# Scores of the local attention issued in pairs of an even and an odd head

## The reference

```
q = q.reshape(B, NC, CHUNK, SWA_KV_HEADS, G, SWA_HEAD_DIM)
...
s = jnp.einsum('bcqkgd,bcjkd->bckgqj', q, kb).astype(jnp.float32) * (SWA_HEAD_DIM ** -0.5)
s = s - slopes[:, :, None, None] * dist
s = jnp.where(valid[None, :, None, None, None, :], s, NEG_INF)
m = jnp.maximum(jnp.max(s, axis=-1, keepdims=True), sink)
p = jnp.exp(s - m)
p = (p / (jnp.sum(p, axis=-1, keepdims=True) + jnp.exp(sink - m))).astype(v.dtype)
o = jnp.einsum('bckgqj,bcjkd->bcqkgd', p, vb)
```

## Time and profile before

| | |
|---|---|
| median of 3 runs | 1539.07 us (1538.87 to 1539.4) |
| the profiled execution's own time | 1538.87 us |
| its span, first to last instruction | 1536.8 us |
| PE busy | 98% |
| DVE busy | 78% |
| ACT busy | 66% |
| busy time of all local scores (line 1494), 64 matmul instructions in the two layers | 272 to 480 ns each |
| attention part with the twelve fills, layer 0 | about 72 to 139 us |
| attention part with the twelve fills, layer 1 | about 436 to 503 us |

### The profile page before, as it was taken

One profiled execution on the slowest core, in us unless ns is written; L12 is line 12 of the kernel. 1 busy time (PEld: TensorE's weight loads), 2 busy tenths in 40 slices (PEclk: granted clock), 3 DMA queues, 4 the chain that ended last, 5 costly groups with the idle time before them and its releaser, 6 DMA issues.

```text
span 1536.8 us, 17866 instructions
## 1 busy us (share of the span) xinstructions
PE 1507.0 (98%) x7188; PEld 1255.9 (82%) x7188; DVE 1195.7 (78%) x965; ACT 1008.9 (66%) x967; POOL 50.5 (3%) x63
## 2 busy tenths in 40 slices
PE   9999999999999989999999999999999999999997
PEld 8888888887888878888888888888888888888885
DVE  5656755656566569888888889889889888898896
ACT  6655544335555467777777777777777777777774
POOL 1000000000000036000000000000000000001000
PEclk9999999999999999999999999999999999999999
DMA  9833465555543439999999999999999999999992
GB/s 352 333 117 110 165 216 185 173 165 179 186 145 117 178 129 411 384 347 400 377 368 386 383 371 370 396 368 371 385 380 369 386 373 369 393 364 373 420 381 101
DMA packets 96487, 460.03 MB, mean 299 GB/s; under 512 B 7656, under 2 KB 13304, under 8 KB 53392
## 3 DMA queue, kind: packets, MB, share of 16 engines
q1 hardware_dynamic: 91632, 444.58, 76.9%
q10 hardware_dynamic: 3312, 9.46, 1.7%
q0 software_dynamic: 1456, 4.79, 0.8%
HBM read 447.79 MB, written 11.01 MB: 299 GB/s over the span
## 4 chain that ended last, share of the span: by engine, by line
PE 93%; DVE 3%; ACT 2%; issue 1%; DMA 1%; SPq 0%; ACTq 0%; DVEq 0%
PE A L430 20%; PE A L432 20%; PE A L431 20%; PE DN L430 8%; PE DN L431 8%; PE DN L432 8%; PE T L1706 2%; PE DN L1518 1%; DVE wlo L405 1%; PE T L432 1%; PE T L430 1%; PE T L431 1%; DMA xs<-in_x 1%; PE A L1494 1%; PE T L1503 1%
## 5 line engine op out<-in xcount | busy, mean ns | idle before, releaser
L405 DVE TENSOR_TENSOR wlo<-raw,whi 128x2048 fp32r<-128x2048 f32 (+2 forms) x335 | 754.0, 2260 | 162.6 <-ACT whi L398 162.2
L398 ACT ACTIVATE whi<-raw 128x2048 fp32r<-128x2048 f32 (+2 forms) x335 | 632.2, 1895 | 217.3 <-PE A L432 122.2
L430 PE MATMUL A<-whi,heTh 128*128 128x512 f32 x672 | 266.3, 396 | 1.2 <-DVE heTl L1247 1.2
L432 PE MATMUL A<-whi,heTl 128*128 128x512 f32 x672 | 262.3, 390 | 0.0
L431 PE MATMUL A<-wlo,heTh 128*128 128x512 f32 x672 | 261.7, 390 | 0.0
L405 DVE TENSOR_TENSOR wlo_more<-raw,whi_more 128x2048 fp32r<-128x2048 f32 x84 | 192.2, 2288 | 40.2 <-ACT whi_more L398 40.0
L398 ACT ACTIVATE whi_more<-raw 128x2048 fp32r<-128x2048 f32 x84 | 161.1, 1918 | 35.6 <-PE A L432 19.6
L430 PE MATMUL A<-whi,hTh 128*128 128x512 f32 (+2 forms) x448 | 174.2, 389 | 3.8 <-DVE hTl L904 1.8
L431 PE MATMUL A<-wlo,hTh 128*128 128x512 f32 (+2 forms) x448 | 169.9, 379 | 0.0
L432 PE MATMUL A<-whi,hTl 128*128 128x512 f32 (+2 forms) x448 | 169.9, 379 | 0.0
L430 PE MATMUL DN<-whi,aTh 128*128 128x512 f32 x376 | 147.9, 393 | 8.2 <-DVE aTl L1266 8.2
(11 more groups left out here) (310 smaller groups left out, 1767.2 us busy)
## 6 DMA issues: line engine op xcount, KB each, us to landing
raw<-in_moe_w_gate SPq DMA_DIRECT2D x112, 1024.0 KB, 7.4
raw<-in_moe_w_up SPq DMA_DIRECT2D x112, 1024.0 KB, 7.5
raw<-in_moe_w_down SPq DMA_DIRECT2D x112, 1024.0 KB, 7.4
raw<-in_w_in SPq DMA_DIRECT2D x22, 1024.0 KB, 7.2
raw<-in_dense_w_down SPq DMA_DIRECT2D x11, 1024.0 KB, 4.8
raw<-in_dense_w_gate SPq DMA_DIRECT2D x10, 1024.0 KB, 5.1
raw<-in_dense_w_up SPq DMA_DIRECT2D x10, 1024.0 KB, 5.1
raw<-in_w_out SPq DMA_DIRECT2D x8, 1024.0 KB, 5.0
```

What stands on the lines that cost most here:

```text
L398: nc.scalar.activation(split_slot(u, e)[0][:, :n], raw[:, u % R, :n], ACT.Copy).then_inc(hi_done, 1)
L405: nc.vector.tensor_tensor(lo[:, :n], raw[:, u % R, :n], hi[:, :n].bitcast(F32), ALU.subtract).then_inc(lo_done, 1)
L430: nc.tensor.matmul(o, hi, wh, start=start, stop=False)
L432: return nc.tensor.matmul(o, lo, wh, start=False, stop=stop)
```

## The change

Fills of the local attention are made in pairs: the list of fills now alternates even heads and odd heads for b = 1 too, so fills 8 to 11 hold heads 0, 2 / 1, 3 / 4, 6 / 5, 7. `scores` serves the latent attention alone. A new function `paired_scores(f)` issues the matmuls of fills f and f + 1 together, in turn one of the even head (partitions 0 to 63, bank A0) and one of the odd head (partitions 64 to 127, bank A1), and signals both at the end. It is called at f = 5 for fills 6 and 7, at f = 6 for fills 8 and 9, and at f = 8 for fills 10 and 11. The programs of ACT and DVE stay as they are, but for which heads stand in fills 9 and 10.

```diff
-        order = list(range(HEADS)) if kind == 0 else list(range(0, HEADS, 2)) + list(range(1, HEADS, 2))
-        FILLS += [(kind, b, order[h:h + per]) for h in range(0, HEADS, per)]
+        step = 1 + kind
+        FILLS += [(kind, b, list(range(h + r, h + r + step * per, step)))
+                  for h in range(0, HEADS, step * per) for r in range(step)]
...
                     if f >= 2:
-                        if FILLS[f - 2][0] == 0:
-                            pe.wait_ge(exp_done[l], EXPS[f - 2])
-                        else:
-                            pe.wait_ge(masked[l], f - 1 - MLA_FILLS)
+                        pe.wait_ge(exp_done[l], EXPS[f - 2])
...
+                def paired_scores(f):
+
+                    b = FILLS[f][1]
+                    w = P * (b + 1)
+                    if f == MLA_FILLS:
+                        pe.wait_ge(exp_done[l], EXPS[f - 1])
+                    else:
+                        pe.wait_ge(masked[l], f - MLA_FILLS)
+                    for i in range(len(FILLS[f][2])):
+                        for side in range(2):
+                            h = FILLS[f + side][2][i]
+                            r = slice(SW_D * side, SW_D * side + SW_D)
+                            last = nc.tensor.matmul(A[(f + side) % 2][:, i * w:(i + 1) * w],
+                                                    sqT[r, h // 2, b * P:(b + 1) * P], skT[r, h // 4, 0:w],
+                                                    start=True, stop=True)
+                    last.then_inc(scored[l], 2)
...
                 for f in range(NF):
                     turn_probs(f)
-                    if f + 2 < NF:
+                    if f + 2 < MLA_FILLS:
                         scores(f + 2)
+                    elif f == MLA_FILLS - 1:
+                        paired_scores(f + 1)
+                    elif f >= MLA_FILLS and f % 2 == 0 and f + 2 < NF:
+                        paired_scores(f + 2)
                     half_unit(f + 2)
```

More of the change, by code:

```diff
@@ L1482, in scores @@
                     if f >= 2:
-                        if FILLS[f - 2][0] == 0:
-                            pe.wait_ge(exp_done[l], EXPS[f - 2])
-                        else:
-                            pe.wait_ge(masked[l], f - 1 - MLA_FILLS)
+                        pe.wait_ge(exp_done[l], EXPS[f - 2])
                     for i, h in enumerate(heads):
                         o = A[f % 2][:, i * w:(i + 1) * w]
[L1489 to L1494, removed]
-                    last.then_inc(scored[l], 1)
+                        last = nc.tensor.matmul(o, qT[0:AUG, h, b * P:(b + 1) * P], kT[0:AUG, h, 0:w],
+                                                start=True, stop=True)
+                    last.then_inc(scored[l], 1)
+                def paired_scores(f):
[11 more added lines that the diff above has]
+                                                    sqT[r, h // 2, b * P:(b + 1) * P], skT[r, h // 4, 0:w],
+                                                    start=True, stop=True)
+                    last.then_inc(scored[l], 2)
                 def turn_probs(f):
```

## The result

The changed kernel takes 1543.5 us (median of 8 runs, 1542.69 to 1544.09) against 1539.05 us for the kernel before on the same chip (8 runs, 1538.87 to 1539.4). The ratio is 1.0027, 95% interval 1.0017 to 1.0038: slower, by 4.45 us. The time lies in the range, but it is 1.6 us above the forecast. The increase of 0.27% is just above the 0.2% that I had called the least that can be told from no change; the interval reaches from 0.17% to 0.38%.

What follows compares the result with a forecast made beforehand. PE, busy 98% of the time, was taken as the bound. Per layer +3.73 (later half unit) - 3.78 (three fills gone) + 1.47 (one pair) = +1.42 us, +2.8 for two layers: 1541.9 us, range 1539.7 to 1544.8.

Steps and rivals of the forecast that it cites:

- the likeliest case: Only the 256-column pairs overlap, full clock: +1.42 us per layer, 1541.9 us in all; chance 0.30.
- rivals 1 and 3: First: 128-column pair overlaps too, 1540.4 us, chance 0.22. Second: clock falls in PE's new idle time, chance 0.15.
- Prices of the steps: PE, local attention: durations read from the old trace put the first pair's start at 101.29 us, from 96.72.
- The chain: From DVE's `mask_max(6)` through ACT and DVE to PE: 9.69 us, so `half_unit(8)` starts 3.73 us later, at 113.06.
- The overlap: Neighbouring matmuls of a pair on different row halves run side by side, saving between nothing and 0.65 or 0.78 us.
- the 256-column pair overlaps, the 128-column one does not: Assumption for PE's paired scores: until the half unit, 1.27 us for 256 columns and 1.98 for 128.
- with order kept, 5 places instead of 8: Upper end for the 8 instructions of a 256-column pair on PE: saves 3 x 0.215 = 0.65 us.
- The clock: PE's clock falling to 1.2 GHz behind the new stall, 2.83 us a layer; left out of the forecast sum.
- Rival 3: Clock falls to 1.2 GHz at `half_unit(8)`, 2.83 us more: one layer 1544.7, both 1547.6 us; chance 0.15.
- decides only from an idle time above 2.23 us on: PE's clock fall could matter only above 2.23 us, the longest idle time in the old trace, which kept full clock.
- Behind the stall: After `half_unit(8)`, three single fills of scores (3.78 us) become one pair of fills 10 and 11, 1.47 us with overlap.
- Rival 5: The chain is covered, `half_unit(8)` starts when PE arrives: 1536.1 to 1532.0 us in all; chance 0.06.

Runs made afterwards that it cites:

- e1_busy_wait: The changed kernel with 16 dummy matmuls of 128 columns filling PE's wait for `gate_add(2)` before `half_unit(8)`; 1539.83 us.
- e4_halves_one_by_one: The changed kernel with, inside each pair, all even heads issued first and then all odd heads; 1545.01 us.

## Why the prediction was right or wrong

The time lies in the range, and the forecast was slightly too low. But the likeliest case was not what happened: rivals 1 and 3 came true together, and their errors in my sum, -2.2 and +4.0 us, partly cancelled. That the time is inside the range is to that extent luck.

- **Prices of the steps: right.** From the transposes of fill 4 to the pair it is 4.57 us, as added up (96.72 to 101.29; measured 97.02 to 101.59). The 0.30 us offset was there before the change's first step.
- **The chain: right.** 9.69 us forecast from `mask_max(6)` to `half_unit(8)`, 9.66 measured (102.80 to 112.46). Each link is in the chain of waits, and taking it out at either of two links gives back the wait. The idle time of 3.5 to 4.2 us was 4.20.
- **The overlap: mis-sized.** The step "the 256-column pair overlaps, the 128-column one does not" failed, and so did "with order kept, 5 places instead of 8". All pairs overlap fully, at 1.09 and 1.07 us until the half unit, where I had 1.98 and 1.27. This is 0.89 + 0.20 us per layer, 2.2 in all. The row I leaned on, the values matmuls at 0.105 us each, does show a limit other than columns, but it doesn't add up across the two halves. Whether the limit is the weight load, as I took as most likely, no run here shows; if it is, the loads of the two halves run side by side, for each of the 16 instructions has one of its own. The rule of the Trainium skill, "TensorEngine Tiling (Array Packing)", Key Properties, that different tiles do their weight loads and their matmuls in parallel, is borne out by this trace: 16 instructions of 128 columns, each with its weight load, in 1.09 us.
- **The clock: the term I set to nothing.** Rival 3 had a chance of 0.15 and a price of 2.83 us per layer, and the sum had nothing for it; measured were 2.13 and 1.59 us, and 0.3 in the router part. It was less than the price because the clock came back within the half unit, and in layer 1 fell only as it began. That it "decides only from an idle time above 2.23 us on" failed: in the changed kernel's profile it also fell behind the router's wait of this length, and in all it fell in or behind this wait in six of the eleven profiles. Five of the eleven ran at the full clock there and took 18.36 or 18.37 us from the end of that wait to the end of the next long one; the six took 18.38 to 19.85. I had read one profile of one execution as the rule. Three executions of the kernel before, of 1540.32 to 1540.79 us, also stand out, with the lowest mean clock of that kernel, 0.996. They weren't profiled; that the same happened in them is likely, but not shown.
- **Behind the stall: right in kind.** 3 x 1.26 us were replaced by one pair, which cost 1.28 instead of 1.47. With this and the overlap (`half_unit(8)` starts 2.83 us later, at 112.46 less the 0.30 of offset against 109.33), a layer would be +2.83 - 3.78 + 1.28 = +0.33 us. `e1_busy_wait`, which is this kernel with both half units at full clock, is 0.7 us above the kernel before, though its interval contains 1. In its profile the two attention parts are 0.26 and 0.32 us longer than before (96.90 to 130.65 and 461.14 to 494.90 us).
- **Rival 5** gave 1532.0 for the case that the chain is covered; both runs that cover it took 1531.2 to 1531.3. It was right that the change as made does not cover it.

What stays open: whether the clock falls at an idle time of 2.2 to 2.9 us differs between profiled executions, and between the two layers of one, and no run here says what it depends on.

## What to carry to other kernels

When work that was issued early is moved later to join a partner, follow the work that is queued behind its consumers on every engine: here the exponentials stood ahead of a weight split that stood ahead of an unrelated read of a bank for which PE waits. Swapping two statements turned 4.45 us lost into 7.8 us gained. Price a new PE wait by the clock too: of the 4.45 us, 3.7 went away with dummy matmuls in the wait.

## What the hardware showed that I had not expected

- Matmuls of 64 rows on the two row halves, into two banks, take half the time of those on one half: 16 instructions of 128 columns in 1.09 us, as long as 8 on one half take, and 8 of 256 columns in 1.07 against 1.92 on one half. This includes their weight loads.
- They need not alternate in the program: with four 256-column instructions of one half ahead of four of the other, the pair still takes 1.07 us. With eight 128-column ones ahead of eight, it takes 1.64, a part of the gain only.
- The granted clock fell in or just behind every one of the four idle times of 4.2 us (changed kernel and `e4_halves_one_by_one`, both layers each), in one of two of 2.90 us, and in or behind the one of 2.23 us in six of eleven profiles. The last cost between nothing and 1.5 us.
